# The second block's norms computed and applied in halves of 512 columns

## What is computed

```python
def rms_norm_2(x, gain):
    xf = x.astype(jnp.float32)
    y = xf * lax.rsqrt(jnp.mean(xf * xf, axis=-1, keepdims=True) + NORM_EPS)
    return (y * gain.astype(jnp.float32)).astype(x.dtype)
...
    h = x
    for l in range(DEPTH):
        u = rms_norm_2(h, attn_pre_norm[l])
        mix = hybrid_mixer(u, w_in[l], ...)
        h = h + rms_norm_2(mix, attn_post_norm[l])
        u = rms_norm_2(h, mlp_pre_norm[l])
        m = jnp.square(jax.nn.relu(u @ w_mlp_up[l])) @ w_mlp_down[l]
        h = h + rms_norm_2(m, mlp_post_norm[l])
    return h
```

## Time and profile before

| | us |
|---|---|
| median of 3 runs | 1250.86 (1246.35 to 1251.92) |
| the profiled execution | 1246.27 |
| its span in the trace | 1244.4 |
| TensorE busy | 1081.4 (87%) |
| VectorE, GpSimd, ScalarE busy | 776.5, 738.3, 462.1 |

### The profile page before, as it was taken

The page is one execution under the profiler, slowest core; times in us unless marked ns, Lnnn a source line. Parts: engine busy times, 40 slices in busy tenths (PEclk is TensorE's granted clock), DMA queues, the critical chain, the costliest instruction groups (busy, mean ns, idle before and its releaser), DMA issues.

```text
span 1244.4 us, 14945 instructions
## 1 busy us (share of the span) xinstructions
PE 1081.4 (87%) x5092; PEld 743.5 (60%) x5092; DVE 776.5 (62%) x1525; ACT 462.1 (37%) x984; POOL 738.3 (59%) x445
## 2 busy tenths in 40 slices
PE   6999988999877778777777777999999997999997
PEld 5877544554423223232232233999989996998996
DVE  2526987769668577685775555414444453867976
ACT  4754332231221211212112123546666435444442
POOL 6354766656434434344443341886697985888884
PEclk9999999999999998999999999899999998999999
DMA  7436999999999999999999996753444553555552
GB/s 270 173 119 273 382 421 420 420 420 421 421 421 421 421 421 416 398 421 421 421 422 421 419 413 264 258 191 110 146 160 144 187 179 135 179 192 188 186 187 84
DMA packets 65810, 372.27 MB, mean 299 GB/s; under 512 B 7592, under 2 KB 8720, under 8 KB 32656
## 3 DMA queue, kind: packets, MB, share of 16 engines
q0 software_dynamic: 36864, 268.45, 52.2%
q1 hardware_dynamic: 27696, 98.07, 23.9%
q10 hardware_dynamic: 1184, 4.88, 1.1%
HBM read 369.79 MB, written 1.06 MB: 298 GB/s over the span
## 4 chain that ended last, share of the span: by engine, by line
PE 49%; DMA 27%; DVE 13%; ACT 5%; issue 3%; POOL 2%; DVEq 0%; SPq 0%; POOLq 0%; ACTq 0%
DMA arena<-in_peer_uv,idx_all 27%; PE ps L1540 12%; PE ps L1273 11%; PE ps L1275 11%; PE ps L1274 11%; DVE arena L1088 5%; POOL w_hl L348 2%; PE ps L1581 1%; ACT prob L574 1%; DVE yT L1246 1%; ACT prob L488 1%; PE ps L1502 1%; DVE wts L1097 1%; DVE arena L1244 1%; ACT w_hl L415 1%
## 5 line engine op out<-in xcount | busy, mean ns | idle before, releaser
L1540 PE MATMUL ps<-arena,prob 128*128 128x512 f32 x1024 | 484.3, 620 | 123.8 <-ACT prob L574 123.3
L348 POOL TENSOR_TENSOR w_hl<-ring,w_hl 128x1024 fp32r<-128x1024 f32 x176 | 443.5, 2529 | 140.3 <-ACT w_hl L415 138.9
L359 POOL DMA_INDIRECT arena<-in_peer_uv,idx_all x256 | 288.6, 1127 | 350.0 <-PE ps L1540 311.2
L1540 PEld LDWEIGHTS ps<-arena,prob 128*128 128x128 f32 x1024 | 190.4, 195 | 406.2 <-ACT prob L574 208.4
L1088 DVE CUSTOM_DVE_ANT_0 arena<-arena,xn 128x1024 f32<-128x1024 f32 x256 | 324.3, 1269 | 152.3 <-DMA arena<-in_peer_uv,idx_all 149.5
L1273 PE MATMUL ps<-xT,w_hl 128*128 128x256 f32 x848 | 245.0, 289 | 5.7 <-DVE xT L809 3.3
L1274 PE MATMUL ps<-xT,w_hl 128*128 128x256 f32 x848 | 241.9, 285 | 0.0
L1275 PE MATMUL ps<-xT,w_hl 128*128 128x256 f32 x848 | 241.9, 285 | 0.0
L415 ACT ACTIVATE w_hl<-ring 128x1024 fp32r<-128x1024 f32 x176 | 185.4, 1057 | 109.1 <-PE ps L1275 102.5
L569 ACT ACTIVATE gel<-acts 128x2 f32<-128x2 f32 x129 | 26.2, 203 | 404.1 <-DVE acts L1088 404.0
L1273 PEld LDWEIGHTS ps<-xT,w_hl 128*128 128x128 f32 x848 | 164.7, 194 | 8.3 <-issue 5.7
(11 more groups left out here) (222 smaller groups left out, 1011.4 us busy)
## 6 DMA issues: line engine op xcount, KB each, us to landing
ring<-in_weights SPq DMA_DIRECT2D x178, 512.0 KB, 3.5
arena<-in_peer_uv,idx_all POOLq DMA_INDIRECT x256, 13.3
arena<-in_rg_weights ACTq DMA_DIRECT2D x1, 2048.0 KB, 9.2
x<-in_x SPq DMA_DIRECT2D x2, 512.0 KB, 4.7
bias<-rel_scratch SPq DMA_DIRECT2D x1, 1024.0 KB, 7.7
arena<-in_subkeys SPq DMA_DIRECT2D x1, 1024.0 KB, 5.7
out_x<-x ACTq DMA_DIRECT2D x2, 512.0 KB, 2.6
arena<-in_band SPq DMA_DIRECT2D x1, 768.0 KB, 9.3
```

What stands on the lines that cost most here:

```text
L348: pool.tensor_tensor(pair[:, 1, :], ring[:, n % RING, :], pair[:, 0, :].bitcast(F32), ALU.subtract).then_inc(w_lo, 1)
L359: pool.indirect_dma_start(uv_slot(n), None, A["peer_uv"], bass.IndirectOffsetOnAxis(idx_all[:, h, c:c + 1], 0))\
L1540: j = pe.matmul(banks(2 + 2 * t + half), diag[:, n % GRING, :], uv_slot(n)[:, D + half * 512:D + (half + 1) * 512], start=False, stop=(h = ...
```

## The change

Tile 1 of norm 2 and both tiles of norms 3, 4 and 5 are worked on in two halves of 512 columns. ScalarE squares the first half into `part_ssq` and makes of it `part_eps` = mean part + eps, which is the bias of the root after the second half. In norms 3 and 5 VectorE multiplies each half of the sums by the gain row in place (`gained`) as soon as that half is squared, and behind the reciprocal one operation per half scales and adds x (`new_x`). The normalised rows are written in halves and `transposes` waits for each. `row_products_by_tile` runs the halves outside and the chunks inside; tile 0's transposes of norm 4 stand ahead of tile 1's last three matmuls. The output leaves in four transfers of 256 KB. Semaphores and four small tensors are added.

```diff
@@ -84,6 +84,24 @@
 def topk_at(h, t):
 
     return (t if h == 0 else h + 1) * TOPK_STAGES
+
+
+def xn_at(k, t, half):
+
+    if k < 2:
+        return 2 * k + t + 1
+    if k == 2:
+        return 5 if t == 0 else 6 + half
+    return 7 + 2 * t + half + 1
+
+
+HALVES = [slice(0, 512), slice(512, 1024)]
+PARTS = [(2, 1), (3, 0), (4, 0), (3, 1), (4, 1), (5, 0), (5, 1)]
+
+
+def part_at(r, t):
+
+    return 2 * PARTS.index((r, t))
 
 
 def norm_at(r, t):
...
@@ -401,8 +422,21 @@
 
             def square_root(r, t):
                 act.wait_ge(sq_done, norm_at(r, t) + 1 if r else 2)
-                act.activation(root[:, t:t + 1], ssq[:, t:t + 1], ACT.Sqrt, bias=eps_col[:],
+                eps = eps_col[:]
+                if (r, t) in PARTS:
+                    act.wait_ge(part_sq, part_at(r, t) + 2)
+                    eps = part_eps[:, t:t + 1]
+                act.activation(root[:, t:t + 1], ssq[:, t:t + 1], ACT.Sqrt, bias=eps,
                                scale=1.0 / D).then_inc(root_done, 1)
+
+            def first_half_square(r, t, src):
+                act.activation(xn[:, t, 0:512], src, ACT.Square, accum_out=part_ssq[:, t:t + 1]).then_inc(part_sq, 1)
+                act.wait_ge(part_sq, part_at(r, t) + 1)
+                act.activation(part_eps[:, t:t + 1], part_ssq[:, t:t + 1], ACT.Identity, bias=eps_col[:],
+                               scale=1.0 / D).then_inc(part_sq, 1)
+
+            def second_half_square(t, src):
+                act.activation(xn[:, t, 512:D], src, ACT.Square, accum_out=ssq[:, t:t + 1]).then_inc(sq_done, 1)
 
             def split_hi(n, i=None, step=8):
 
@@ -560,8 +594,14 @@
                                    accum_out=exs[:, h % 2, t:t + 1]).then_inc(ex_done, 1)
 
             def x2_square(t):
-                act.wait_ge(v_used, PH * SLOTS - (NT - 1 - t) * TOPK)
-                act.activation(xn[:, t, :], banks(2 + 2 * t, 2), ACT.Square, accum_out=ssq[:, t:t + 1]).then_inc(sq_done, 1)
+                if t == 0:
+                    act.wait_ge(v_used, PH * SLOTS - TOPK)
+                    act.activation(xn[:, 0, :], banks(2, 2), ACT.Square, accum_out=ssq[:, 0:1]).then_inc(sq_done, 1)
+                else:
+                    act.wait_ge(first_half_done, 1)
+                    first_half_square(2, 1, banks(4))
+                    act.wait_ge(v_used, PH * SLOTS)
+                    second_half_square(1, banks(5))
 
             def weights(n, count, turn):
 
@@ -732,25 +772,32 @@
                 split_hi(n)
 
             load_root_table()
-            def sums_square(n, t, last):
-
+            def first_sums(n, t):
+                act.wait_ge(sums_done, 1 + 3 * n + 2 * t + 1)
+                first_half_square(3 + 2 * n, t, banks(4 + 2 * t))
+
+            def second_sums(n, t, last):
                 if t == 0:
-                    act.wait_ge(sums_done, n + 2)
+                    act.wait_ge(sums_done, 1 + 3 * n + 2)
                 else:
                     act.wait_ge(w_used, last)
-                square_sum(t, banks(4 + 2 * t, 2))
+                second_half_square(t, banks(5 + 2 * t))
                 square_root(3 + 2 * n, t)
 
             def new_x_square(t):
+                act.wait_ge(post_step, 2 * t + 1)
+                first_half_square(4, t, x[:, t, 0:512])
                 act.wait_ge(post_step, 2 * t + 2)
-                act.activation(xn[:, t, :], x[:, t, :], ACT.Square, accum_out=ssq[:, t:t + 1]).then_inc(sq_done, 1)
+                second_half_square(t, x[:, t, 512:D])
                 square_root(4, t)
 
-            sums_square(0, 0, W_OUT2 + 8)
+            first_sums(0, 0)
+            second_sums(0, 0, W_OUT2 + 8)
             split_hi(W_MLP)
             new_x_square(0)
-            sums_square(0, 1, W_OUT2 + 8)
+            first_sums(0, 1)
             evac_xT(3, 0, C_MP)
+            second_sums(0, 1, W_OUT2 + 8)
             new_x_square(1)
             act.dma_start(row_gain[:], A["mlp_post"].broadcast_to([P, D])).then_inc(row_ld, 16)
             split_hi(W_MLP + 1)
@@ -772,11 +819,13 @@
 
             load_root_table()
             for t in range(NT):
-                sums_square(1, t, W_END)
+                first_sums(1, t)
+                second_sums(1, t, W_END)
             for t in range(NT):
-                act.wait_ge(post_step, 4 + 2 * t + 2)
-                act.dma_start(out[t], x[:, t, :]).then_inc(out_st, 16)
-            act.wait_ge(out_st, 16 * NT)
+                for half in range(2):
+                    act.wait_ge(post_step, 4 + 2 * t + half + 1)
+                    act.dma_start(out[t][:, HALVES[half]], x[:, t, HALVES[half]]).then_inc(out_st, 16)
+            act.wait_ge(out_st, 16 * NT * 2)
 
 
 
@@ -795,6 +844,10 @@
                 else:
                     dve.tensor_scalar(xn[:, t, :], x[:, t, :] if src is None else src, rinv[:, t:t + 1], None,
                                       ALU.mult).then_inc(xn_done, 1)
+
+            def normalised_halves(t, src):
+                for at in HALVES:
+                    dve.tensor_scalar(xn[:, t, at], src[:, at], rinv[:, t:t + 1], None, ALU.mult).then_inc(xn_done, 1)
 
             def split_lo(pair, c, src):
 
@@ -1137,7 +1190,7 @@
                     make_gates(h + 1)
 
             rstd(2, 1)
-            normalised(1, banks(4, 2))
+            normalised_halves(1, banks(4, 2))
             evac_xT(2, 1, C_AP)
             keep_sums(1)
 
@@ -1221,22 +1274,34 @@
                 dve.wait_ge(merged_done, 3 * m + 2)
                 split_lo(yT, m, both).then_inc(merged_done, 1)
 
-            def post_norm(r, n, t):
+            def gained(r, n, t, half):
+
+                if half == 0:
+                    dve.wait_ge(part_sq, part_at(r, t) + 1)
+                else:
+                    dve.wait_ge(sq_done, norm_at(r, t) + 1)
+                sums = banks(4 + 2 * t + half)
+                dve.tensor_tensor(sums, sums, row_gain[:, HALVES[half]], ALU.mult).then_inc(gained_done, 1)
+
+            def new_x(r, n, t):
                 rstd(r, t)
-                sums = banks(4 + 2 * t, 2)
-                dve.scalar_tensor_tensor(out=sums, in0=sums, scalar=rinv[:, t:t + 1],
-                                         in1=row_gain[:], op0=ALU.mult, op1=ALU.mult).then_inc(post_step, 1)
-                dve.wait_ge(post_step, 4 * n + 2 * t + 1)
-                dve.tensor_tensor(x[:, t, :], x[:, t, :], sums, ALU.add).then_inc(post_step, 1)
+                dve.wait_ge(gained_done, 4 * n + 2 * t + 2)
+                for half, at in enumerate(HALVES):
+                    dve.scalar_tensor_tensor(out=x[:, t, at], in0=banks(4 + 2 * t + half), scalar=rinv[:, t:t + 1],
+                                             in1=x[:, t, at], op0=ALU.mult, op1=ALU.add).then_inc(post_step, 1)
 
             dve.wait_ge(row_ld, 32)
-            post_norm(3, 0, 0)
+            for half in range(2):
+                gained(3, 0, 0, half)
+            new_x(3, 0, 0)
             rstd(4, 0)
-            normalised(0)
-            post_norm(3, 0, 1)
+            normalised_halves(0, x[:, 0, :])
+            gained(3, 0, 1, 0)
             evac_xT(3, 0, C_MP)
+            gained(3, 0, 1, 1)
+            new_x(3, 0, 1)
             rstd(4, 1)
-            normalised(1)
+            normalised_halves(1, x[:, 1, :])
             evac_xT(3, 1, C_MP)
             with dve.Fori(0, 4) as i:
                 for m in range(8):
@@ -1248,15 +1313,18 @@
                     split_lo(yT, m, hid[:, m, :]).then_inc(hid_done, 1)
             dve.wait_ge(row_ld, 48)
             for t in range(NT):
-                post_norm(5, 1, t)
+                for half in range(2):
+                    gained(5, 1, t, half)
+                new_x(5, 1, t)
 
 
         @block.tensor
         def _(pe):
             def transposes(k, t):
 
-                pe.wait_ge(xn_done, 2 * k + t + 1)
                 for c in range(NC_):
+                    if c % 4 == 0:
+                        pe.wait_ge(xn_done, xn_at(k, t, c // 4))
                     i = pe.transpose(tr_banks(k, t)[:, c * P:(c + 1) * P],
                                      xn[:, t, c * P:(c + 1) * P], ident[:])
                     if c % 4 == 3:
@@ -1317,16 +1385,21 @@
                     i = matmul3(banks(4 + 2 * t + half), lhs, parts(w, slice(half * 512, (half + 1) * 512)), False, last)
                 return i
 
-            def row_products_by_tile(weights, lhs, ready):
+            def row_products_by_tile(weights, lhs, ready, near_end=None):
 
                 for t in range(NT):
-                    for n, (w_at, chunk) in enumerate(weights):
-                        ready(chunk, t)
-                        i = half_rows(w_at, lhs(chunk, t), t, n == len(weights) - 1)
-                        if t == 1:
-                            i.then_inc(w_used, 1)
-                    if t == 0:
-                        i.then_inc(sums_done, 1)
+                    for half in range(2):
```

(19 more changed lines are left out.)

3 lines of the change are left out of this document (added).

## The result

| | median us (lowest to highest, runs) | against before, 95% interval |
|---|---|---|
| before | 1247.92 (1245.00 to 1251.92, 20) | |
| changed kernel | 1254.75 (1250.74 to 1257.96, 20) | 1.0048 (1.0038 to 1.0059) |

The change makes the kernel 6.0 us slower (4.7 to 7.4, the ratio by 1247.9). The profiled execution took 1255.51 with a span of 1253.7 us; before it was 1246.27 and 1244.4. One execution of experiment 6 took 3430.54 us; the median and ratio given there are of its other eleven.

A forecast was written before the change was run, and what follows sets the result against it. Chain: TensorE 49%, gathers 27%; second-block norms count only where all of TensorE waits for them. Terms -0.5 + 4.9 + 0.2 + 1.7 = +6.3 on the median 1250.86 gave 1257.1 us, range 1249 to 1262.5.

The forecast's parts named there:

- Place A: Second tile's norm after the peer stage: normalising releases the transposes after 0.75 instead of 1.29, so -0.5 us.
- Place B: Output projection to MLP: TensorE waits for chunk 7's weights, ScalarE's weight split delays the square of new x; +4.9 us.
- The stall: Output projection: TensorE asks for chunk 7's weights at 1034.8 and waits for GpSimd's split until 1036.8, 2.0 us late.
- the late split: Before the MLP: ScalarE's split of the first MLP matrix waits for chunk 4, ends at 1044.9; new x's square queues behind.
- GpSimd beside VectorE: Before the MLP: tile 0's normalising halves on VectorE wait for GpSimd's half of the weight split, +0.3 us.
- Place C: The end: products 2.0 us later, new x +0.8, last transfer saves 0.6; net +0.2 us.
- The output in halves: Output tail: last transfer has half the bytes and saves 0.6 us; by the skill's batching rule it would save nothing.
- The clock: TensorE's granted clock halves after new stalls, chance one in four at B, two in three at C; one fall, +1.7 us.
- 1 (no fall): Rival: the stalls at B and C come without a fall of TensorE's clock, +4.6, 1255.5 us; chance 0.25.
- 2 (the inputs are there): Rival: chunk 7's weights and the hidden chunk are ready in time and the halves gain, -3.8, 1247.1 us; chance 0.10.
- 3 (ScalarE is not held up): Rival: weight split doesn't delay new x's square; B about +2.2, total +3.6, 1254.5 us; chance 0.10 together with rival 4.
- 4: Rival: later waits take back gains and losses, nothing moves, 1250.9 us; chance 0.10 together with rival 3.

The follow-up runs named there:

- experiment 6: Experiment 5's kernel with ScalarE's split of the first MLP matrix moved behind tile 0's new-x square and tile 1's first half square: 1245.04 us, 0.9964 of before.
- experiment 4: Changed kernel with ScalarE's split of the first MLP matrix moved behind tile 0's new-x square and tile 1's first half square: 1251.37 us, 1.0026 of before.
- 3: Changed kernel with both halves of a chunk taken together for tile 0 only, tile 1 still half by half: 1249.95 us, 1.0001 of before.
- 2: Changed kernel with TensorE's old order put back (both halves of a chunk together, both tiles), norms still in halves: 1244.80 us, 0.9978 of before.
- 5: Changed kernel, old chunk order at output projection, at the end for tile 0 only; tile 0's evacuation split and moved behind tile 1's second square: 1243.66 us, 0.9954.
- 1: Kernel before with only TensorE's half order (first 512 columns of all chunks, then the second), norms whole: 1257.08 us, 1.0066 of before.
- 11: Kernel before with only TensorE's half order, norms whole, the same edit as experiment 1 measured again: 1257.97 us, 1.0085 of before.
- Experiment 8: Experiment 5's kernel with each output tile leaving in one 512 KB transfer instead of two halves: 1246.74 us in one execution.

## Why the prediction was right, step by step

The range held the time and the sign was right. The sum was +6.3; by A, B and C it is +5.6 and +5.8, in two executions that both had the one fall that the sum counts. Without a fall it would be about +4.1 (A -0.9, B +4.8, C +0.2 from experiment 4), and with three falls in five about +5, which the interval of the ratio (4.7 to 7.4) holds too. That both profiled executions had the fall is luck in their close fit to the sum. The forecast of 1257.1 is 2.4 above the measured median; setting the sum on the median of three runs (1250.86) where twenty give 1247.92 accounts for more than that, 2.9.

- **Place A, predicted -0.5, measured -0.9** (waits of 2.22 to 2.35 in ten executions with halves, against 3.14 in four without). The step that failed is the start of the second square: I put it 0.5 behind the last peer product (773.85 against 773.34), and it came 0.1 behind it. The first half's sums were ready 0.8 before that product ended, not 0.43. ScalarE's timeline of the changed kernel; the last peer product ends at 777.35:

```profile
776.53 0.60 ACT L433 ACTIVATE xn<-ps 128x512 f32<-128x512 f32 x1 [0.34 <-PE ps L1613]
...
777.45 0.58 ACT L439 ACTIVATE xn<-ps 128x512 f32<-128x512 f32 x1
```

- **Place B, predicted +4.9, measured +4.8 and +4.8.** The stall was 1.75 of shown idle for 2.0 of delay. Its parts: without the late split -2.0 (experiment 4), with chunk order for tile 0 -2.0 (3), for both tiles -4.0 (2), and with the evacuation moved as well -7.0 (5, which changes several things at once). The forecast's "split at 1043.8, square at 1044.9" reads 1046.77 and 1047.73 in the trace, where the whole place starts 2.8 later; with that shift, the marks of its chain that the rows above show, down to the MLP's first product, are met within 0.2.
- **GpSimd beside VectorE, predicted +0.3, measured +0.2.** Normalising tile 0 took 1.09 beside GpSimd's split and 0.88 for tile 1 without it; in experiment 4, with the split elsewhere, tile 0 took 0.88 too. This agrees with the exclusive lock of the Trainium skill (SBUF — State Buffer, SBUF: two separate sides) as to who waits. The size hangs on how much of the split is left when VectorE comes: 0.42 us here. In experiments 1 and 11 it was 0.94, and normalising 1024 columns took 1.50 and 1.48 instead of 0.75. In all three VectorE ended 0.2 us earlier than if it had waited for the recorded end of the split. Experiment 11's timelines of GpSimd and VectorE:

```profile
1048.38 2.36 POOL L348 TENSOR_TENSOR w_hl<-ring,w_hl 128x1024 fp32r<-128x1024 f32 x1 [8.56 <-ACT w_hl L415]
...
1049.80 1.48 DVE L796 TENSOR_SCALAR xn<-x,rinv 128x1024 f32<-128x1024 f32 x1
```

- **Place C, predicted +0.2 without a fall.** Stall +2.0 (13.4 us from C's beginning to the last matmul in experiments 4 and 1, against 11.5; predicted 2.0); from the last matmul to the last new x 3.36 instead of 4.65, so -1.3 (predicted -1.2); output tail -0.5 (predicted -0.6). Net +0.2, as C says in experiment 4 (19.33 against 19.12). The halves do gain at the end; the order spends it.
- **The output in halves.** The Trainium skill (DMA: Bandwidth & Descriptors, Bandwidth) advises to batch transfers, and I took from it that the tail would not shrink. That was more than the advice says: it is about the share of the peak rate. Experiment 8 shows 0.5 us for the halves: at the end of a program the last transfer's own length counts, not the rate.
- **The clock, predicted one fall, +1.7.** At the end 3 falls in 5, where I gave two chances in three, at 1.5 to 1.6 each. At chunk 7's stall none in 5, where I gave one in four. The falls behind tile 0's transposes were not in the forecast, and they are free.
- **Rivals.** 1 (no fall) has the same mechanism as the forecast and is what the executions without a fall do; the times alone don't tell how many of the 20 those are. 2 (the inputs are there) is refuted by the two waits. 3 (ScalarE is not held up) is refuted by the 2.44 us wait of the split and by experiment 4. 4 fell with the ratio. What 2 offered, -3.8 us if the inputs were there in time, is shown in part: the halves with the old order bring -2.7 us (experiment 2), and -5.7 with the evacuation placed anew (5).
